# Attention scores of the first model in two rounded passes, with keys and queries split right after their projection

## The reference, cut to what matters

```python
h, hc = norm(x) * (1 + scale) + shift, norm(xc) * (1 + cscale) + cshift
...q, k, v of two attentions = split_proj(h @ w_in), and of the context from hc @ w_in
# "window": 4 query heads, 2 key heads of 64, keys within 128 tokens plus the context, a learned sink
s   = einsum(qb, kw) * 64 ** -0.5           # context scores beside it
p   = softmax(concat([s_loc, s_ctx, sink]))[..., :-1]
o   = p_loc @ vw + p_ctx @ vc
# "global": the same heads over all 768 keys, q and k normalized per head first
p   = softmax(einsum(q, kall) * 64 ** -0.5);  o = p @ vall
x   = x + g1 * (concat([ya, yb, yc, yd]) @ w_out)      # ya, yb: two convolution mixers
x   = x + g2 * expert_choice_ffn(norm(x) * (1 + sc2) + sh2)   # 16 experts
```

## Time and profile before

| | |
|---|---|
| median of 3 runs | 3169.51 us |
| the profiled execution, as timed | 3187.95 us |
| its span in the trace | 3186.1 us |
| mean granted TensorE clock | 0.963 of full speed |
| PE busy | 2972.8 us, 93% of the span |
| PEld, DVE, ACT, POOL busy | 1871.4, 1105.2, 738.3, 384.3 us |
| DMA | 627.05 MB, mean 197 GB/s |
| of it POOL's queue q0 | 46.27 MB, 4.4% of the 16 engines' time |

### The profile page before, as it was taken

How to read it: one execution, slowest core, us unless ns; L and a number is a source line. 1 busy time by engine, 2 the same in 40 slices (tenths; PEclk the granted TensorE clock), 3 DMA queues, 4 the chain that set the end, 5 groups by cost and what they waited for, 6 DMA issues and landing times.

```text
span 3186.1 us, 50032 instructions
## 1 busy us (share of the span) xinstructions
PE 2972.8 (93%) x21634; PEld 1871.4 (59%) x21634; DVE 1105.2 (35%) x1948; ACT 738.3 (23%) x1393; POOL 384.3 (12%) x497
## 2 busy tenths in 40 slices
PE   6999986999999898996988888999999999999998
PEld 3655555645545464553443335888865568678887
DVE  4134854111111343743322224223344463222232
ACT  3113651000000233630000003222223352222232
POOL 2023521122212121501000000000000000000000
PEclk9998998999999998997999999999999989999999
DMA  9930044999999610039999994211311202232130
GB/s 381 367 125 1 1 164 172 383 409 400 403 408 399 243 56 1 1 152 392 423 423 423 423 422 163 106 66 68 123 60 54 80 8 80 79 113 81 52 146 27
DMA packets 138512, 627.05 MB, mean 197 GB/s; under 512 B 12640, under 2 KB 19872, under 8 KB 83008
## 3 DMA queue, kind: packets, MB, share of 16 engines
q1 hardware_dynamic: 122064, 577.67, 45.3%
q0 software_dynamic: 16240, 46.27, 4.4%
HBM read 607.45 MB, written 16.45 MB: 196 GB/s over the span
## 4 chain that ended last, share of the span: by engine, by line
PE 43%; DMA 10%; DVE 2%; ACT 1%; issue 1%; SPq 0%; POOL 0%; DVEq 0%; ACTq 0%; POOLq 0%
PE bank L979 20%; DMA slots<-in_w_up_dram 8%; PE bank L1559 8%; PE bank L1747 4%; PE bank L1436 3%; PE bank L1663 3%; DMA slots<-in_w_gate_dram 2%; PE bank L1303 2%; PE bank L1680 1%; PE bank L1457 1%; PE bank L1691 1%; PE bank L1681 0%; PE bank L1486 0%; PE bank L1080 0%; PE bank L1081 0%
## 5 line engine op out<-in xcount | busy, mean ns | idle before, releaser
L1436 PE MATMUL bank<-slots,HT 128*32 128x256 f32 x8192 | 492.4, 387 | 49.1 <-DMA slots<-in_w_gate_dram 24.4
L1436 PEld LDWEIGHTS bank<-slots,HT 128*32 128x32 f32 x8192 | 274.8, 112 | 270.0 <-issue 76.6
L979 PE MATMUL bank<-hT_high,chunk_high 128*128 128x512 f32 (+2 forms) x736 | 285.2, 388 | 5.7 <-DVE hT_low L2535 5.7
L979 PE MATMUL bank<-hT_high,low_slots 128*128 128x512 f32 (+2 forms) x736 | 287.1, 390 | 0.0
L979 PE MATMUL bank<-hT_low,chunk_high 128*128 128x512 f32 (+2 forms) x736 | 285.6, 388 | 0.0
L2129 ACT ACTIVATE arena<-bank 128x512 f32<-128x512 f32 x32 | 19.2, 598 | 771.8 <-PE bank L1436 433.3
L2908 DVE TENSOR_TENSOR arena<-bank,arena 128x512 f32<-128x512 f32 x32 | 22.1, 692 | 457.8 <-ACT arena L2129 457.8
L979 PE MATMUL bank<-slots,HT 128*128 128x512 f32 (+4 forms) x544 | 176.7, 483 | 1.4 <-ACT done_mark L2385 1.4
L979 PEld LDWEIGHTS bank<-hT_high,chunk_high 128*128 128x128 f32 x736 | 139.0, 189 | 36.7 <-DVE hT_low L2535 6.1
L979 PEld LDWEIGHTS bank<-hT_low,chunk_high 128*128 128x128 f32 x736 | 138.9, 189 | 32.1 <-issue 0.2
L979 PEld LDWEIGHTS bank<-hT_high,low_slots 128*128 128x128 f32 x736 | 138.8, 189 | 29.4
(11 more groups left out here) (462 smaller groups left out, 4857.5 us busy)
## 6 DMA issues: line engine op xcount, KB each, us to landing
slots<-in_w_gate_dram SPq DMA_DIRECT2D x128, 1024.0 KB, 10.0
slots<-in_w_up_dram SPq DMA_DIRECT2D x128, 1024.0 KB, 12.1
arena<-in_w_down_dram SPq DMA_DIRECT2D x80, 1024.0 KB, 26.4
arena<-in_ada_w_dram SPq DMA_DIRECT2D x48, 1024.0 KB, 8.6
X<-in_w_down_dram SPq DMA_DIRECT2D x32, 1024.0 KB, 9.0
slots<-in_w_in_dram SPq DMA_DIRECT2D x15, 2048.0 KB, 8.6
slots<-in_ffn_w_gate_dram SPq DMA_DIRECT2D x10, 2048.0 KB, 7.9
slots<-in_ffn_w_up_dram SPq DMA_DIRECT2D x10, 2048.0 KB, 8.1
```

The source lines that it names most:

```text
L979: mm = pe.matmul(out_, lhsT, rhs, start=(n == 0), stop=(n == len(pairs) - 1))
L1436: mm = pe.matmul(bank[32 * j:32 * j + 32, 2 + n, 256 * g:256 * g + 256], xT[:, 64 * k + 32 * g:64 * k + 32 * g + 32], columns(w[:, c, :], ...
```

## The change

It has six parts.

1. The scores are two fp32r passes. The first multiplies `k_round` (rounded keys, 64 rows and the row of ones) with `q_high` (rounded queries and the shift). The second has 128 rows: `k_stack` (high keys above, low keys below) with `q_stack` (low queries above, high queries below), so that high x low and low x high are added in one pass. The row scores use `k_stack`'s high rows and `q_high`.
2. For this, `qkv` splits each tile on DVE after the rotation: a rounded copy `qk_high` and the difference, both 128x768 (keys only for layer 1's context: 512 wide). PE turns the high part with a rounded identity as a matmul and the low part by the transposes of before. The low turn of tile i-2 stands inside the projection of tile i. ACT copies the high parts (12 copies a tile instead of 8), DVE the low parts (8 copies a tile). Banks 6 and 7 are used twice a tile.
3. The rounding of the queries at the start of `attend` is gone; that of the keys stays, but only the scores wait for it.
4. The row of ones is written by DVE at the start of `attend`, ahead of the maxima; POOL's long memsets of one row in `qkv` are gone, and POOL's memsets of the sink rows go to the start of `attend`. The mix of the sink waits for POOL's first tap as well.
5. ACT copies the shift first and makes the sink's exponentials from the copy.
6. `q_stack` of layer 0 lies in the memory of `X`. The residual's six DMAs move from the start of `qkv` to the start of `conv_out`, ahead of the modulation loads.

```diff
 stage qkv, PE
+                def turned(i, low):
+                            if low:
+                                mm = pe.transpose(bank[:, 6 + kind, tile_cols(c)], qk_tok[:, i % 2, cols], ident[:, :])
+                            else:
+                                mm = pe.matmul(bank[:, 6 + kind, tile_cols(c)], qk_high[:, i % 2, cols], ident_round[:, :],
+                                               start=True, stop=True)
...
                         product(bank[:, b + j, lo:hi], [(HT[:, k, tile_cols(i)], w[:, k, lo:hi]) for k in range(KD)],
                                 sem[f"full{b}"] if j else None)
+                        if j == 0 and between is not None:
+                            turned(between, 1)
...
                     if i:
-                        turned(i - 1)
+                        turned(i - 1, 0)
+                last = ST + CT - 1
+                if VALUES_LAST[st.layer] > last:
+                    turned(last - 1, 1)
                 for i in range(VALUES_LAST[st.layer], ST + CT):
-                    project(i, 2, 384, 512)
-                turned(ST + CT - 1)
+                    project(i, 2, 384, 512, last - 1 if i == VALUES_LAST[st.layer] else None)
+                turned(last, 0)
+                turned(last, 1)
 stage attend, PE: row scores, then scores
-                    if unit is group.units[0] and group.main:
-                        pe.wait_ge(sem["rounded"], st.at("rounded", 2 * mains))
-                    kT = k_round[st.layer][0:HD + 1, group.kind, group.g, :]
-                    q = q_round[st.layer][0:HD + 1, group.kind, group.heads + unit.j, tile_cols(qt)]
+                    kT = k_stack[0:HD, group.kind, group.g, :]
+                    q = q_high[st.layer][0:HD, group.kind, group.heads + unit.j, tile_cols(qt)]
...
                     if one.first:
+                        pe.wait_ge(sem["rounded"], st.at("rounded", mains))
                         pe.wait_ge(sem["shift_done"], st.at("shift_done", group.number + 1))
-                    keys = K_ext[0:HD + 1, group.kind, group.g, tile_cols(one.kt)]
+                    keys = k_round[st.layer][0:HD + 1, group.kind, group.g, tile_cols(one.kt)]
+                    both_keys = k_stack[:, group.kind, group.g, tile_cols(one.kt)]
...
-                        mm = pe.matmul(bank[:, b, 0:one.hi - one.lo], keys, q_ext[0:HD + 1, ..., one.lo:one.hi],
-                                       start=True, stop=not near)
+                        pe.matmul(bank[:, b, 0:one.hi - one.lo], keys, q_high[st.layer][0:HD + 1, ..., one.lo:one.hi],
+                                  start=True, stop=False)
+                        mm = pe.matmul(bank[:, b, 0:one.hi - one.lo], both_keys, q_stack[st.layer][:, ..., one.lo:one.hi],
+                                       start=False, stop=not near)
 stage qkv, ACT: take_turned
+                                act.activation(q_high[...][0:HD, kind, heads, tile_cols(i)], turned[rows, 0:2, :], ACT.Copy)
+                                act.activation(q_stack[...][HD:2 * HD, kind, heads, tile_cols(i)], turned[rows, 0:2, :], ACT.Copy)
+                            ins = act.activation(k_stack[0:HD, kind, g, tile_cols(i)], turned[rows, 2, :], ACT.Copy)
 stage attend, ACT
-                    act.activation(q_round[...][0:HD + 1, kind, 2 * g:2 * g + 2, :], q_ext[..., 0:SEQ], ACT.Copy)
 stage qkv, DVE: a tile's end, and take_low at the head of tile i + 2
+                            if l == 0 or i < ST:
+                                dve.tensor_copy(q_stack[l][0:HD, kind, heads, tile_cols(i)], turned[rows, 0:2, :])
+                            ins = dve.tensor_copy(k_stack[HD:2 * HD, kind, g, tile_cols(i)], turned[rows, 2, :])
...
-                    ins.then_inc(sem["qk_ready"], 1)
+                    step(ins)
+                    step(dve.tensor_copy(qk_high[:, i % 2, cols], qk_tok[:, i % 2, cols]))
+                    dve.tensor_tensor(qk_tok[:, i % 2, cols], qk_tok[:, i % 2, cols], qk_high[:, i % 2, cols].bitcast(F32), ALU.subtract)\
+                       .then_inc(sem["qk_ready"], 1)
 stage attend, DVE
+                dve.memset(key_ones(l), 1.0)
                 for group in groups[:ahead]:
 stages qkv and conv_out, POOL
             def qkv(st):
-                for t in range(ST + CT if st.layer == 0 else 0):
-                    pool.dma_start(X[:, t, :], residual_rows(t)).then_inc(sem["x_again"], 16)
-                step(pool.memset(K_ext[HD:HD + 1, :, :, :], 1.0))
-                step(pool.memset(Q_ext(st.layer)[HD:HD + 1, :, :, :], 0.0))
...
             def conv_out(st):
+                for t in range(ST + CT if st.layer == 0 else 0):
+                    pool.dma_start(X[:, t, :], residual_rows(t)).then_inc(sem["x_again"], 16)
                 for row in range(mod_kinds(st.layer)):
```

91 lines of the change are left out of this document (51 added, 40 removed).

## The result

The changed kernel takes 3225.88 us (median of 4 runs, 3218.81 to 3233.44) against 3169.24 us: a ratio of 1.018, with a 95% interval of 1.0154 to 1.0205. The forecast was 3177.5 with a range of 3158 to 3190: the sign was right, the size was off by 48 us.

What follows compares the result with a forecast made beforehand. The prediction took PE's own order as the path, with short waits for other engines at its seams. Its terms, -16 - 10 + 8 + 6 + 18 + 2 = +8 us, took 3169.51 to 3177.5 us, range 3158 to 3190.

Steps and rivals of the forecast that it cites:

- The steady step of attend: One step of `attend`, 4.14 us before, would take 3.6 us with a wait for DVE of about 0.3 in it.
- A pair of 512 and 256: In `attend`, a pair of row scores of 512 and 256 columns costs PE about 0.33 us.
- The walk through the groups: `attend` followed with PE's new step length and the others' old one: -16 us in layer 0, -10 in layer 1.
- The clock: Further stretches of PE at the half level, as faster scores leave it idle more often: +2 us (0 to 6).
- the sign that I had named: In the new profile, a granted clock of 0.8 in `attend`, instead of near 0.93, would point to the clock.
- The loads of conv_out: In `conv_out`, PE waits 16 us for small loads behind the residual's, plus 2 for slow clock: +18 us.
- The broadcasts as a second line: If small loads are not held, DVE in `w_out` awaits broadcasts behind the residual: about +5 us for PE; chance 0.14.
- qkv: Splitting tiles in `qkv` costs +8 us in layer 0 (5 to 11) and +6 in layer 1 (3 to 9).
- a tail of 0.9: At the end of layer 0's `qkv`, tile 5's two successive turns, with extra ACT and DVE copies: +0.9 us.
- The start of attend: DVE's memset of ones ahead of the first maximum takes 2.6 us; layer 0's start still gains 3.4.
- The forecast's case: The whole kernel at 3177.5 us, with an own range of 3170 to 3186; chance 0.50.
- The rival of the clock: Holes in each `attend` step drop the clock: 25 us at half level cost some 12; sum +20, 3189.5 us; chance 0.18.

Runs made afterwards that it cites:

- Experiment 5: The kernel before the change, with the row scores' two operands cut from 65 rows to 64: 3200.85 us, ratio 1.0092.
- experiment 6: The changed kernel, with the row scores over 65 rows again (first low key times a row of zeros): 3196.64 us.
- Experiment 4: The changed kernel, with two DVE taps instead of five ahead of the next group's maxima: 3215.53 us.
- experiments 1: The kernel before the change, with only the residual's six loads moved to the start of layer 0's `conv_out`: 3184.35 us, ratio 1.0061.
- experiment 2: The changed kernel, with the two small modulation loads of `conv_out` issued ahead of the residual's six: 3211.67 us.
- Experiment 7: The changed kernel, with the last low and high turns in layer 0's `qkv` spread over the last values' projections: 3220.55 us.
- experiment 9: The changed kernel with 65-row row scores, spread turns, two taps and small loads first, plus the row of ones written by POOL: 3165.05 us.

## Why the prediction was wrong

By the marks, the miss lies in three places: 12.9 us in layer 0's `attend`, 29.2 in layer 1's, and 10.9 in the two `qkv`. The two `attend` were to bring -26 and cost +16; so the sign came out right by the loads and `qkv`, and not by what I said of attention.

**The steady step of attend is the first step that failed.** "A pair of 512 and 256 is about 0.33" was worked out from rounded products over 128 rows. It fits the row scores before, which had 65 rows, and was carried over to row scores of another shape. I read the diff as leaving them alone but for their tile names; it cut `[0:HD + 1]` to `[0:HD]`. Experiment 5 puts the price of that cut at 32 us in the kernel before, experiment 6 at 29 in the changed one, some 16 of them through layer 1's clock. In steady steps it comes to 0.78 and 0.41 us (less in the changed kernel, where part of it covered the wait for DVE): 4.15 us a step, where I had 3.6. The Trainium skill says in one line ("TensorEngine Tiling (Array Packing)", section "Key Properties") that a change of the array's tiling mode drains TensorE. It lists tiles of 64 rows as a mode, but doesn't say that operands of 64 rows bring it about. The traces agree with it as far as they go: a pass over 128 rows follows one over 65 after 0.23 us, and between 64 rows and either of them about 0.2 us is added. They show the late weight load; that it is a drain is my reading. I had not looked there, since I took the shape for the same.

**The walk through the groups** was right in kind once that is out, and too hopeful by a third: 3.74 us a step with 0.28 of wait for DVE, against 3.6 and 0.30; -11.0 and -6.3 in `attend` against -16 and -10. PE's waits at the mixes for what ACT takes out came to 12.3 us in layer 0's `attend` of experiment 6, against 6.1 before.

**The clock is the second term that failed.** I had it as 2 us, and as a rival at 12 by holes in every step. It took about 18 us of layer 1's `attend` alone (64.8 us at the half level instead of 28.5; granted clock 0.77, and 0.8 was the sign that I had named for this rival). But it came by a route I didn't name: a single wait of 2.05 us for DVE behind five taps, and then 31 us at 1.2 GHz. Experiment 4 takes the wait away and gets 12 us back. Experiment 6 makes the stretch go too, without touching the taps, but it also cuts that wait to 0.94 us, so it doesn't tell whether the 64-row matmuls helped to keep TensorE slow. Waits of 0.91 (before) and 0.94 us at this boundary were followed by no such stretch, the wait of 2.05 us by one in each of three traces. (A wait of 1.77 us for ACT stands 8 us ahead of it, but one of 1.80 does so in experiment 6 too.) Why it lasts 31 us with PE at work all the time stays open.

**The loads of conv_out** were right, in mechanism and size: 16 us of wait forecast, 14.79 measured, +18 against +18.2 with `w_out`. The prediction took its rule on the order within a queue from the Trainium skill ("DMA: Bandwidth & Descriptors", section "Queues, rings and completion order"), and the trace before had no case of it. The section tells of the order within a ring for the DMAs of SP and ACT; here the queue is POOL's, and experiments 1 and 2 agree with the rule: PE waits 14.57 us for the small loads when they are issued behind the residual's, and not at all when they are issued first. The broadcasts as a second line (5 us in the rival) measured 7.1.

**qkv** was under-sized, in the mechanism named. Layer 0: high matmuls 4.0, waits for ACT 3.2 and a tail of 0.9 made 8; the waits were 8.7 in all, because tile 5's two turns stand behind each other with the same waits as tile 4's, and not with 0.9. Experiment 7 removes 5.8. Layer 1: 6 forecast, 11.1 measured, with 6.2 us of wait for ACT and 1.8 for DVE where 3.3 for DVE stood before; I can't assign all of the rest.

**The start of attend**: memset 2.62 us against 2.6, on the path, as experiment 9 shows by taking it off.

**The chances.** The forecast's case got 0.50 with a range that ended at +21 us. None of my rivals reached +57: they varied the terms I had, one at a time, and the price of a row score was a quantity I held for unchanged. The rival of the clock, at +20, had the right size for layer 1 and the wrong way there.

## What to carry to other kernels

When a diff touches a slice of a matmul's operand, write down rows and columns of both operands before and after, also for the matmuls that the change isn't about; here 64 rows between matmuls of 65 and 128 cost 0.39 us a pair of row scores (experiment 5), more than the 0.33 that I had for the pair itself. When one engine's step gets shorter, look at each boundary for the engine that used to be just in time, since the wait of 2.05 us cost 12 here, with what the clock took. And put small loads that someone waits for ahead of large ones that nobody needs yet.

## What the runs showed of the hardware

- A rounded matmul of 512 columns over 64 rows, put between matmuls over 65 or 128: its weight load starts with it, 0.08 us before its predecessor's recorded end, and a pair of 512 and 256 columns takes 0.54 us. One row more takes 0.41 us off a step of 4.15 with two such pairs (experiment 6), one row less adds 0.78 to a step of 4.14 (experiment 5). Where a matmul over 128 rows stands between two row scores of 64 rows (window attention, 256 columns each), they start 0.31 us apart in the changed kernel and 0.12 with 65 rows (experiment 6).
- TensorE stayed at 1.2 GHz (0.50 granted) for 31 us with PE busy in 30.42 of them, behind a wait of 2.05 us; in three traces of the same code alike.
- The same `attend` of layer 0 was at the half level for 38.9, 41.3 and 59.7 us in three profiled executions with the same instructions there (experiment 2, the changed kernel, experiment 7).
- A DVE memset of 3072 elements on one partition takes 2.62 us, as the 1.44 us for 1656 on 128 partitions had suggested.
